# A decoder step with routed experts: expert table made first, gathers and weights issued at other places

## What is computed

```
mod = silu(c) @ w_mod + b_mod                       # six rows of scales, shifts and gates per sequence
h   = rms_norm(x) * (1 + scale1) + shift1
p   = h @ w_in                                      # columns for RWKV heads, a gated MLP, attention
x   = x + gate1 * (concat(rwkv, gmlp, attention) @ w_out)
h2  = rms_norm(x) * (1 + scale2) + shift2
# experts: 4 groups of 4; top group, then the top 2 experts in it
pg  = softmax(h2 @ rg_w + rg_b);  g_idx = argmax(pg)
pe  = softmax((h2 @ re_w + re_b) of the group);  e_idx = top 2;  gate = pg_top * pe_top / sum(pe_top)
hid = silu(h2 @ wg[e]) * (h2 @ wu[e])               # only the two chosen experts of a token count
x   = x + gate2 * sum over the two of gate * (hid @ wd[e])
y   = rms_norm(x) * final_g
```

## Time and profile before

| | us |
|---|---|
| timed runs, median of 3 (lowest, highest) | 1572.51 (1571.71, 1573.48) |
| the profiled execution: its own time, its span | 1567.69, 1565.7 |
| PE busy in matmuls, of the span | 1342.6 (86%) |
| DVE, ACT, POOL busy | 623.9, 424.5, 132.6 |
| DMA | 191.68 MB, 122 GB/s mean |

### The profile page before, as it was taken

The page is one execution under the profiler, slowest core; times in us unless marked ns, Lnnn a source line. Parts: engine busy times, 40 slices in busy tenths (PEclk is TensorE's granted clock), DMA queues, the critical chain, the costliest instruction groups (busy, mean ns, idle before and its releaser), DMA issues. The chain is left out here.

```text
span 1565.7 us, 29065 instructions
## 1 busy us (share of the span) xinstructions
PE 1342.6 (86%) x10641; PEld 773.6 (49%) x10641; DVE 623.9 (40%) x1214; ACT 424.5 (27%) x860; POOL 132.6 (8%) x338
## 2 busy tenths in 40 slices
PE   5999899989999999977868898699953999899945
PEld 2554555445353535245546888544422555555512
DVE  4202537613636262743332566522344222222217
ACT  3101134114636363733421222201120111111113
POOL 0100110001011110100000000040000111000031
PEclk9999999999999999989987999899975999999978
DMA  9202123721010101246733000081004768746774
GB/s 348 90 0 74 30 85 98 268 83 42 1 41 1 41 1 45 78 162 226 258 109 121 17 4 3 4 237 41 27 34 162 261 211 301 274 159 241 277 262 178
DMA packets 87507, 191.68 MB, mean 122 GB/s; under 512 B 17995, under 2 KB 41042, under 8 KB 77811
## 3 DMA queue, kind: packets, MB, share of 16 engines
q1 hardware_dynamic: 74004, 158.09, 29.2%
q0 software_dynamic: 6256, 20.71, 3.9%
q10 hardware_dynamic: 7152, 11.55, 2.3%
HBM read 163.01 MB, written 27.31 MB: 122 GB/s over the span
## 5 line engine op out<-in xcount | busy, mean ns | idle before, releaser
L2706 PE MATMUL ex_ps_g<-all_mT,ex_xt 128*64 128x256 f32 x1344 | 157.2, 387 | 17.3 <-DMA all_mT<-in_exp_wu 15.8
L2706 PEld LDWEIGHTS ex_ps_g<-all_mT,ex_xt 128*64 128x64 f32 x1344 | 97.6, 139 | 64.4 <-issue 11.8
L1699 PE MATMUL at_ps_z<-all_hT,mix_v_g 128*128 128x363 f32 (+1 forms) x384 | 120.9, 473 | 4.4 <-PEq L105 4.4
L2333 PE MATMUL op_ps_o<-all_hT,op_m_t 128*128 128x512 f32 x256 | 115.8, 608 | 7.9 <-POOL op_m_t L2313 7.9
L576 PE MATMUL rp_ps<-all_hT,mix_rp_w 128*128 128x384 f32 (+1 forms) x336 | 109.4, 481 | 4.1 <-PEq L105 4.1
L1848 DVE TENSOR_SCALAR at_zc<-at_ps_z,at_bias 128x512 f32<-128x512 f32 (+3 forms) x96 | 54.5, 612 | 134.8 <-PE at_ps_z L1715 134.0
L1699 PEld LDWEIGHTS at_ps_z<-all_hT,mix_v_g 128*128 128x128 f32 x384 | 72.9, 192 | 51.1 <-issue 9.8
L341 PE MATMUL fr_big<-all_mT,all_hT 128*128 128x256 f32 (+3 forms) x288 | 94.9, 493 | 3.0 <-DVE all_hT L394 3.0
L576 PEld LDWEIGHTS rp_ps<-all_hT,mix_rp_w 128*128 128x128 f32 x336 | 63.7, 194 | 51.0 <-issue 16.5
L2723 PE MATMUL ex_ps_y<-all_hT,ex_hid_T 128*64 128x512 f32 x336 | 80.5, 599 | 2.0 <-issue 1.2
L2333 PEld LDWEIGHTS op_ps_o<-all_hT,op_m_t 128*128 128x128 f32 x256 | 48.6, 194 | 66.2 <-issue 57.9
(11 more groups left out here) (478 smaller groups left out, 2030.5 us busy)
## 6 DMA issues: line engine op xcount, KB each, us to landing
all_mT<-in_exp_wg SPq DMA_DIRECT2D x17, 1024.0 KB, 4.8
all_mT<-in_exp_wu SPq DMA_DIRECT2D x17, 1024.0 KB, 8.0
all_hT<-in_exp_wd SPq DMA_DIRECT2D x17, 1024.0 KB, 7.4
all_hT<-in_cache_k SPq DMA_DIRECT2D x64, 256.0 KB, 3.9
sa_v<-in_cache_v SPq DMA_DIRECT2D x64, 256.0 KB, 4.3
slot_rows<-ex_y ACTq DMA_DIRECT2D x84, 128.0 KB, 5.3
mix_v_g<-in_w_mod SPq DMA_DIRECT2D x8, 1024.0 KB, 5.0
rp_w_mod<-in_w_mod SPq DMA_DIRECT2D x8, 1024.0 KB, 5.7
```

Source lines behind the costliest of these rows:

```text
L1699: last = nc.tensor.matmul(third(x_, c), w[:, x_, k, :], hT[:, k, lo:hi], start=(k == 0), stop=(k == KT - 1))
L2333: last = nc.tensor.matmul(ps_o[0:m, u, lo:lo + 512], m_t[:, u, k, 0:m], w[:, k, lo:lo + 512], start=(k == 0), stop=(k == KT - 1))
L2706: final = nc.tensor.matmul(ps_g[rows, u, 0:DE], xt[:, k, HALVES[u]], w1[:, u, x_, k, :], start=(k == 0), stop=(k == KT - 1))
```

## The change

Five edits:
- Front: the value columns go in two passes over the tiles, first the 256 columns of all nine, then the 512 columns of all nine; the weights of the two have a semaphore each, and so have the finished tiles (`g_done`, `v_done`).
- Routing: the steps for the expert of each unit come before those for the slots, and `routed` is raised in between; the number of units used is taken from the last expert's first unit and its count. The token tables are made in two shares, five tiles and four, and PE starts on the first share when that is there (`SHARES`, `HOT`). The cast to `slots` comes last.
- Weights: w1 is loaded in halves of the blocks k, 512 KB for each DMA. The first half waits for `gu_half` (PE's first 8 matmuls of the unit that used the buffer), the second for `gu_done`; in `gate_up` PE waits for the first half at its start (`w1_loaded`) and for the second at block 4 (`w1_rest`).
- The 18 gathers stand at the end of POOL's list of the experts' phase, behind waits for all stores (`all_stored`, `zeros_stored`); `final_rows` and the semaphores `gathered` live on through both phases.

The diff, cut to its core:

```diff

-                pe.wait_ge(wv_loaded, 32)
+                def values(n, col, lo, hi, kept, done):
+                    m = rows_of(n)
+                    if n >= 2:
+                        pe.wait_ge(kept, n - 1)
+                    for k in range(KT):
+                        last = nc.tensor.matmul(big[0:m, n % 2, col:col + hi - lo], hT[:, k, n * P:n * P + m], wv[:, k, lo:hi],
+                                                start=(k == 0), stop=(k == KT - 1))
+                    last.then_inc(done, 1)
+
+                pe.wait_ge(wv_loaded[0], 16)
                 for n in range(NT + 1):
-                    m = rows_of(n)
                     if n == NT:
                         pe.wait_ge(s["s_ready"], 1)
                     elif n % (NT // 2) == 0:
                         pe.wait_ge(s["h_by_dve"], (n // (NT // 2) + 1) * BY_DVE)
                         pe.wait_ge(s["h_by_act"], (n // (NT // 2) + 1) * (KT - BY_DVE))
-                    if n >= 2:
-                        pe.wait_ge(s["vg_kept"], n - 1)
-                        pe.wait_ge(s["vs_kept"], n - 1)
-                    for col, lo, hi in ((0, 0, GW), (512, GW, GW + SBW)):
-                        for k in range(KT):
-                            last = nc.tensor.matmul(big[0:m, n % 2, col:col + hi - lo], hT[:, k, n * P:n * P + m], wv[:, k, lo:hi],
-                                                    start=(k == 0), stop=(k == KT - 1))
-                    last.then_inc(s["v_done"], 1)
+                    values(n, 0, 0, GW, s["vg_kept"], s["g_done"])
+                pe.wait_ge(wv_loaded[1], 16)
+                for n in range(NT + 1):
+                    values(n, 512, GW, GW + SBW, s["vs_kept"], s["v_done"])

...
-    PICKED, PLACED, HOT, EXPERT = 34, 54, 61, 68
+    PICKED, EXPERT, PLACED, HOT = 34, 54, 60, (66, 69)
+    SHARES = ((0, 5), (5, N))
...
                 def load_w1(u, r):
+                    def load_half(e, half, loaded):
+                        ks = slice(half * (KT // 2), (half + 1) * (KT // 2))
+                        for x_, name in enumerate(("exp_wg", "exp_wu")):
+                            sp.dma_start(w1[:, u, x_, ks, :],
+                                         T[name][bass.ds(e, 1), :, :].squeeze(0).rearrange("(p k) f -> p k f", k=KT)[:, ks, :]).then_inc(loaded, 16)
+
                     def load(e):
-                        for x_, name in enumerate(("exp_wg", "exp_wu")):
-                            sp.dma_start(w1[:, u, x_, :, :],
-                                         T[name][bass.ds(e, 1), :, :].squeeze(0).rearrange("(p k) f -> p k f", k=KT)).then_inc(w1_loaded[u], 16)
-
-                    wait_apart(sp, s["gu_done"], r * 2 + u + 1, s["passed"])
-                    unless_held(u, r, load, lambda: sp.sem_inc(w1_loaded[u], 32))
+                        load_half(e, 0, w1_loaded[u])
+                        wait_apart(sp, s["gu_done"], r * 2 + u + 1, s["passed"])
+                        load_half(e, 1, w1_rest[u])
+
+                    def skip():
+                        sp.sem_inc(w1_loaded[u], 32)
+                        wait_apart(sp, s["gu_done"], r * 2 + u + 1, s["passed"])
+                        sp.sem_inc(w1_rest[u], 32)
+
+                    wait_apart(sp, s["gu_half"], r * 2 + u + 1, s["passed"])
+                    unless_held(u, r, load, skip)

...
+                pool.wait_ge(s["all_stored"], 2)
+                pool.wait_ge(zeros_stored, (ROUNDS - 1) * 16)
+                for n in range(N):
+                    m = rows_of(n)
+                    for c in range(2):
+                        nc.gpsimd.indirect_dma_start(token_rows(keep, n)[0:m, c, :], None, slot_rows, bass.IndirectOffsetOnAxis(
+                            ap=slots[0:m, n * 2 + c:n * 2 + c + 1], axis=0)).then_inc(keep["gathered"][n], 16)
...
-                pe.wait_ge(did, HOT)
                 for n in range(N):
+                    for part, (lo, hi) in enumerate(SHARES):
+                        if n == lo:
+                            pe.wait_ge(did, HOT[part])
                     for c in range(2):
...
+                pe.sem_inc(s["gu_half"], 2)
...
                     for k in range(KT):
+                        if k == KT // 2:
+                            pe.wait_ge(w1_rest[u], r * 32 + 32)
                         for x_, rows in enumerate(HALVES):
                             final = nc.tensor.matmul(ps_g[rows, u, 0:DE], xt[:, k, HALVES[u]], w1[:, u, x_, k, :], start=(k == 0), stop=(k == KT - 1))
+                        if k == KT // 2 - 1:
+                            final.then_inc(s["gu_half"], 1)
                     final.then_inc(s["gu_done"], 1)
...
+                step(V.tensor_tensor(cmp3[:, :, :], bc(tiles_at[:, :], 2, NE), bc(first[:, :], 1, EU), ALU.is_ge))
+                step(V.tensor_reduce(expert_f[:, 0:EU], cmp3[:, :, :], axis=AXX, op=ALU.add))
+                step(V.tensor_scalar(expert_f[:, 0:EU], expert_f[:, 0:EU], -1.0, None, ALU.add))
+                step(V.tensor_tensor(used[:, :], first[:, NE - 1:NE], tiles[:, NE - 1:NE], ALU.add))
+                step(V.tensor_tensor(cmp4[:, :], used[:, :].to_broadcast([P, EU // 2 - 1]),
+                                     tiles_at[:, :].rearrange("p (t u) -> p t u", u=2)[:, 1:, 0], ALU.is_gt))
+                step(V.tensor_reduce(expert_f[:, EU:EU + 1], cmp4[:, :], axis=AXX, op=ALU.add))
+                step(V.tensor_copy(unit_expert[:, :], expert_f[:, :]))
+                assert count[0] == EXPERT + 1, count[0]
+                dve.sem_inc(keep["routed"], 1)
+
                 by_choice = lambda ap: ap.rearrange("p e n -> p n e")
                 step(V.tensor_tensor(place[:, :, :], by_choice(run[:, :, 0:2 * N]), by_choice(ps_before), ALU.subtract))
                 step(V.scalar_tensor_tensor(place[:, :, :], bc(first[:, :], 1, 2 * N), float(UNIT), place[:, :, :], ALU.mult, ALU.add))
                 step(V.tensor_tensor(place[:, :, :], place[:, :, :], chosen[:, :, :], ALU.mult))
                 step(V.tensor_reduce(slot_f[:, :], place[:, :, :], axis=AXX, op=ALU.add))
                 step(V.tensor_copy(slot_i[:, :], slot_f[:, :]))
-                step(V.tensor_copy(slots[:, :], slot_f[:, :]))
                 assert count[0] == PLACED, count[0]

                 step(V.tensor_scalar(part_i[:, 0, :], slot_i[:, :], LOG_UNIT, None, ALU.logical_shift_right))
                 step(V.tensor_scalar(part_i[:, 1, :], slot_i[:, :], UNIT - 1, None, ALU.bitwise_and))
                 step(V.tensor_copy(part_f[:, :, :], part_i[:, :, :]))
-                step(V.tensor_tensor(row_hot[:, :, :], bc(part_f[:, 1, :], 2, UNIT), bc(rows_at[:, :], 1, 2 * N), ALU.is_equal))
-                step(V.tensor_tensor(unit_token[:, :, :], bc(part_f[:, 0, :], 2, EU), bc(tiles_at[:, :], 1, 2 * N), ALU.is_equal))
-                for c in range(2):
-                    mine = unit_token[:, :, :].rearrange("p (n c) u -> p n c u", c=2)[:, :, c, :]
-                    step(V.tensor_tensor(mine, mine, bc(token_f[:, :], 2, EU), ALU.mult))
-                assert count[0] == HOT, count[0]
-
-                step(V.tensor_tensor(cmp3[:, :, :], bc(tiles_at[:, :], 2, NE), bc(first[:, :], 1, EU), ALU.is_ge))
-                step(V.tensor_reduce(expert_f[:, 0:EU], cmp3[:, :, :], axis=AXX, op=ALU.add))
-                step(V.tensor_scalar(expert_f[:, 0:EU], expert_f[:, 0:EU], -1.0, None, ALU.add))
-
-                step(V.tensor_reduce(used[:, :], tiles[:, :], axis=AXX, op=ALU.add))
-                step(V.tensor_tensor(cmp4[:, :], used[:, :].to_broadcast([P, EU // 2 - 1]),
-                                     tiles_at[:, :].rearrange("p (t u) -> p t u", u=2)[:, 1:, 0], ALU.is_gt))
-                step(V.tensor_reduce(expert_f[:, EU:EU + 1], cmp4[:, :], axis=AXX, op=ALU.add))
-                step(V.tensor_copy(unit_expert[:, :], expert_f[:, :]))
-                assert count[0] == EXPERT, count[0]
-                dve.sem_inc(keep["routed"], 1)
+                for part, (lo, hi) in enumerate(SHARES):
+                    at, m = slice(2 * lo, 2 * hi), 2 * (hi - lo)
+                    V.tensor_tensor(row_hot[:, at, :], bc(part_f[:, 1, at], 2, UNIT), bc(rows_at[:, :], 1, m), ALU.is_equal).then_inc(did, 1)
+                    V.tensor_tensor(unit_token[:, at, :], bc(part_f[:, 0, at], 2, EU), bc(tiles_at[:, :], 1, m), ALU.is_equal).then_inc(did, 1)
+                    count[0] += 2
+                    dve.wait_ge(did, count[0])
+                    mine = unit_token[:, at, :].rearrange("p (n c) u -> p n c u", c=2)
+                    step(V.tensor_tensor(mine, mine, bc(bc(token_f[:, lo:hi], 2, 2), 3, EU), ALU.mult))
+                    assert count[0] == HOT[part], count[0]
+                step(V.tensor_copy(slots[:, :], slot_f[:, :]))
...
+def token_rows(keep, n):
+
+    of_tile = lambda t, at: t[:, :, :].rearrange("p k t -> p (k t)")[:, at * 2 * D:(at + 1) * 2 * D].rearrange("p (c d) -> p c d", c=2)
```

(21 more changed lines are left out.)

8 lines of the change are left out of this document (3 added, 5 removed).

## The result

The changed kernel took 1582.5 us, the median of five runs (1580.76 to 1586.52), beside 1571.71 for five runs of the kernel before: a ratio of 1.0078, 95% interval 1.0049 to 1.0106. That is 10.8 us slower; forecast were 1581 and a range of 1575 to 1589. The profiled execution has a span of 1579.2 us, 13.5 more than the one of before.

The account below looks back on a forecast made before the run. It took PE to bound the experts' stretch, with w1 waits costing 17.5 us, and a tile-by-tile chain the combining. Terms 24.7 - 16.0 + 0 + 0 = 8.7 gave 1576.4 profiled, 1581 as median, range 1575 to 1589.

Parts of the forecast that it names:

- Part 1: Gathers at the end of the experts' phase: PE starts the combining 25.3 us later, plus 24.7 in all.
- met only when its gathers have landed: End of experts' phase: POOL's drain holds the meeting until its gathers land; 0.7 us taken from landing to drain's end.
- second rival: End of experts' phase: POOL's drain doesn't wait for landings, weights give all; plus 3.2, 1576 us; chance 0.13.
- third rival: End of experts' phase: POOL's meeting passes while gathers are still being issued; -0.7 - 16.0, 1556 us; chance 0.04.
- Part 2: Experts' stretch, w1 in halves: shorter waits for w1 and less slow clock, minus 16.0 us, at most 17.5.
- 3.6 us of slack: w1 loads: first half goes 1.8 us earlier, second is needed 1.8 later, against a longest wait of 2.08.
- What is late next is the down weights: Experts' stretch: down weights, queued behind w1, come earlier only as w1 does; tightest units may keep up to 1 us.
- first rival: w1 loads: halves don't pay, 14 waits shrink about 0.4 us each, the part gives some 8; 1589 us; chance 0.13.
- Part 3: Routing, early expert table and token tables in shares: between 1.2 us later and 1.5 earlier, taken as 0.
- Part 4: Front, value columns in two passes: same matmuls without a gap, copies stay hidden; 0 us.
- Sum: Whole kernel: 24.7 - 16.0 + 0 + 0 = 8.7 us slower, 1581 us as median; chance 0.70.

Follow-up runs that it names:

- e2: Kernel before with only the 18 gathers moved to the end of POOL's experts' phase: 1596.9 us, ratio 1.0192.
- e4: Changed kernel, but only the first tile's two gathers stay in the experts' phase, the other 16 back in the combining: 1559.9 us, ratio 0.9923.
- e1: Changed kernel with the 18 gathers back in the combining, behind the meeting: 1556.4 us, ratio 0.9917.
- e3: Kernel before with only w1 loaded in halves: 1555.7 us, ratio 0.9899.
- e5: Changed kernel with gathers back in the combining, and SP reading the experts ahead of its waits: 1551.1 us, ratio 0.9877.
- e6: Changed kernel with gathers back in the combining, and SP's loop of zeros begun at the first round that can be unused: 1552.6 us, ratio 0.9886.
- e10: Changed kernel with gathers back, experts read first, short zeros loop, and PE's first counts ahead of its token matmuls: 1546.0 us, ratio 0.9843.
- e8: Kernel before with only the value columns in two passes and the new routing: 1569.8 us, ratio 1.0005.

## Why the prediction was right, and where it was off

Right in sign, in the main mechanism and in the time. Its steps:

**Part 1, plus 24.7.** Right. The drain, "met only when its gathers have landed", held in e2, e4 and the changed kernel; e4 excludes the two other readings, that of the second rival among them, and the third rival (the meeting overtakes the gathers) would have left the gap at 18. The gap grew by 24.1 and the combining shrank by 0.85, 23.3 together; e1 says 26.0 and e2 23.0. Within it the drain ended 1.64 after the landing where 0.7 was taken, the train ran from 1495.53 to 1523.73, 28.2 us in place of 29.3, and SP was at the meeting 9.2 us behind PE's last matmul, 10.3 before.

**Part 2, minus 16.0.** Right in direction and in what shortens the waits, but this is the term that was mis-sized: minus 10.3 in the profiled execution, by the stretch. In the two traces: waits for w1 -11.9 (15.8 to 3.9), the slow unit of the earlier trace rows -1.7, waits for down weights +1.8, the wait ahead of the second-last `down` +0.4 (1.2 to 1.6), and the first two units +1.2 (9.72 against 8.51), together -10.2. The 1.2 are not the halves' own, since e3 has 8.54 there: the granted clock rose from 0.5 to 1.0 (from 1.2 to 2.4 GHz) 5.3 us after PE's first `gate_up` began, 2.8 us before the change and 2.9 in e3. Why it rose later stays open.

How far the term was off is less sure than this one pair says: the mean of the experts' stretch is 290.1 us in the three kernels with w1 in one piece and 277.1 in the five with halves as in the change, 13.0 less, and e3's median is 15.8 lower.

The step that failed shows in the loads themselves. It is "3.6 us of slack". It counted the 1.8 us by which the first half goes earlier for the second half too, and that one waits for all of `gate_up`, as the whole load had: it went 0.64 sooner (0.99 us after the `gate_up` in place of 1.63) and took 0.5 longer, so the load was complete 10.0 us after the `gate_up`, and 10.1 before (medians of 15 loads). All that the halves gave is that the end of a load is needed 1.84 us later. e5 takes SP's reading out of the way: complete after 8.6, and all waits are gone. "What is late next is the down weights" was right (1.8 us).

The first rival was nearer here than I allowed, though not by its mechanism: a load took 10.1 us from its first issue, 1.1 of them SP's, where it had 11.6; the longest wait, 2.37, followed a second half of 11.95. That rival's own sum was off by a little too: 14 times 0.4 and 1.7 are 7.3 and not 8, which makes 1590. Nor is there a sign of 4.0 us more for each load: without SP's 1.1 a load took 9.0 us, where it took 8.5 in two pieces. The waits for w1 were forecast under 2 us and came to 3.9 (0.8 to 3.1 in e1, e3, e4 and e6).

**Part 3, 0.** Off by little, with luck in the 0.5 by which PE's first `gate_up` came later in the span: the counting matmuls stood 0.9 earlier in this execution, and the front, forecast "as long as before", grew by 1.4. PE's token matmuls began 1.4 late, the gather of x was issued 1.0 late (1.2 forecast), and it gave nothing back but took 0.4 more (1194.41 to 1203.78, 9.4 us from issue to use, 9.0 before). The smaller pieces beside it didn't let it through in anything near 6.3. Right that SP's early table is held at PE's count; e10 shows that even without that the early table is worth 0.6, and its front of 31.6 is still no shorter than with the old routing (31.1 to 31.5). So the early table gained nothing in any run.

**Part 4, 0.** Right within what can be seen: PE's matmuls of the value columns take 95.29 us from first to last, 94.95 before, so 0.3 more. No run has the value columns alone.

**Sum.** 8.7 forecast; 13.5 between the two profiled executions, 10.8 between the medians. The 4.8 that the sum is short are part 2's 5.7 and part 3's 0.5, less the 1.4 by which part 1 with the combining cost less than 24.7. So that the median came within 1.5 us of 1581 is in part luck: two errors went against each other, and the medians differ by 2.7 less than the two profiled executions do, which is the scatter of single executions.

## What to carry to other kernels

Work that is moved ahead of a meeting of engines must be through before anyone passes it, and for POOL's gathers through means landed (here the drain ended 0.7 to 1.6 us behind the last landing): look in the trace for the drain's end beside the last landing before you fill the time ahead of a barrier with transfers. To get work out of a gap, first ask which engine reaches the meeting last and what it does there: here SP walked through 16 empty passes, 5 us of the gap. And a prefetch that is split goes only as early as its issuer is free: put everything that doesn't depend on the wait (here two table reads, 1.2 us) ahead of it.

## What the runs showed that I had not expected

- POOL's drain kept its distance to the last landing, and not to the last instruction. Behind the 18 gathers in the combining it ended 0.78 us after the landing in all nine kernels that have them there, and 4.5 to 5.8 after the last gather's instruction. In the same nine the drain behind the last gather of x ended 0.91 us after the landing, and 6.3 to 9.5 after the instruction. At the end of the experts' phase it was 1.64 in the changed kernel and e2, and 0.99 in e4. What in POOL holds the drain no run shows. It starts in the trace well before the last gather's instruction does (1503.4 against 1516.72).
- An empty pass of SP's loop with its comparison takes 0.56 us: 20 marks from 1477.9 to 1488.6 in e1.

```profile
L2648 SPq EVENT_SEMAPHORE  x20: 17/17/17, 1477.9 to 1488.6; - x20
```

- After a wait of 2.1 to 2.6 us PE ran a part of the next unit at a granted clock of 0.5 (1.2 GHz) in some executions and not in others. It did so once in the profile of the kernel before (wait 2.08), three times in e8's (2.09, 2.09 and 2.19; 1.5 to 1.7 us each) and once in e3's (2.62; half a `gate_up` took 3.05 us in place of 1.95). The granted clock stayed at 1.0 (2.4 GHz) behind a wait of 2.07 in the kernel before, 2.37 in the changed one, and 2.26 and 2.43 in e2, where the `gate_up` took its usual 3.67:

```profile
1351.08 3.67 PE L2713 MATMUL ex_ps_g<-all_mT,ex_xt 128*64 128x256 f32 x32 [2.43 <-DMA all_mT<-in_exp_wu]
```

So the length of the wait alone doesn't tell it. A part of the scatter between executions is there.
